# Modulation and the first projection chunks at the start of a two-block fp32 transformer kernel: x and ctx loaded first, modulation matmuls in runs of four groups, and half a chunk more of the projection beside them

## The reference

```python
silu_c = jax.nn.silu(c); silu_cc = jax.nn.silu(c_ctx)
mod = silu_c @ w_mod[l] + b_mod[l]
shift, scale, gate = jnp.split(mod[:, None, :], 3, axis=-1)
cmod = silu_cc @ w_mod[l] + b_mod[l]
cshift, cscale, cgate = jnp.split(cmod, 3)
h = rmsnorm(x, norm_g[l]) * (1.0 + scale) + shift
hc = rmsnorm(cx, norm_g[l]) * (1.0 + cscale) + cshift
u = h @ e_w_in[i]
uc = hc @ e_w_in[i]
```

## Time and profile before

| | |
|---|---|
| median of three runs | 2389.93 us |
| the profiled execution | 2389.53 us |
| its span, first to last instruction | 2387.7 us |
| TensorE matmul busy | 2344.4 us, 98% |
| DVE, ACT, POOL busy | 63%, 44%, 11% |
| granted TensorE clock, mean | 0.996 |

### The profile page before, as it was taken

One profiled execution on the slowest core, in us unless ns is written; L12 is line 12 of the kernel. 1 busy time (PEld: TensorE's weight loads), 2 busy tenths in 40 slices (PEclk: granted clock), 3 DMA queues, 4 the chain that ended last, 5 costly groups with the idle time before them and its releaser, 6 DMA issues. The chain is left out here.

```text
span 2387.7 us, 31243 instructions
## 1 busy us (share of the span) xinstructions
PE 2344.4 (98%) x11532; PEld 1901.8 (80%) x11532; DVE 1502.4 (63%) x2492; ACT 1046.8 (44%) x1755; POOL 270.0 (11%) x404
## 2 busy tenths in 40 slices
PE   6999999999999999999999999999999999999998
PEld 1587888877778788877878889878888888998887
DVE  1379655577777888767646566685675544544655
ACT  3332333344443222524544445445454445654543
POOL 0002120121100000011121001010110001101200
PEclk8999999999999999999999999999999999999999
DMA  9968554444435666575565556765655676667653
GB/s 369 370 219 285 177 162 138 156 168 159 142 115 173 233 198 216 174 266 194 167 214 155 164 194 180 239 212 172 210 171 193 187 222 205 199 190 246 187 196 134
DMA packets 234280, 474.79 MB, mean 199 GB/s; under 512 B 18826, under 2 KB 43720, under 8 KB 233360
## 3 DMA queue, kind: packets, MB, share of 16 engines
q1 hardware_dynamic: 208592, 394.42, 51.0%
q0 software_dynamic: 25248, 77.83, 10.1%
q10 hardware_dynamic: 288, 0.52, 0.1%
HBM read 438.77 MB, written 33.94 MB: 198 GB/s over the span
## 5 line engine op out<-in xcount | busy, mean ns | idle before, releaser
L2301 PE MATMUL pp<-w_hi,hT_hi 128*128 128x512 f32 (+4 forms) x2520 | 1004.1, 398 | 0.5 <-DVE w_lo L1657 0.5
L1657 DVE TENSOR_TENSOR w_lo<-raw,w_hi 128x1024 fp32r<-128x1024 f32 (+4 forms) x568 | 669.8, 1183 | 478.6 <-ACT w_hi L1355 477.1
L2303 PE MATMUL pp<-w_hi,hT_lo 128*128 128x512 f32 (+4 forms) x2520 | 964.2, 383 | 0.0
L2302 PE MATMUL pp<-w_lo,hT_hi 128*128 128x512 f32 (+4 forms) x2520 | 962.4, 382 | 0.0
L1355 ACT ACTIVATE w_hi<-raw 128x1024 fp32r<-128x1024 f32 (+4 forms) x568 | 578.8, 1023 | 444.8 <-PE pp L2303 320.3
L2301 PEld LDWEIGHTS pp<-w_hi,hT_hi 128*128 128x128 f32 x2520 | 474.3, 188 | 101.2 <-issue 23.1
L2303 PEld LDWEIGHTS pp<-w_hi,hT_lo 128*128 128x128 f32 x2520 | 473.3, 188 | 88.8
L2302 PEld LDWEIGHTS pp<-w_lo,hT_hi 128*128 128x128 f32 x2520 | 474.8, 188 | 80.3 <-issue 4.6
L1761 DVE SCALAR_TENSOR_TENSOR arena<-raw,cT,arena 128x512 f32<-128x512 f32 x240 | 170.9, 747 | 1.9
L2296 PE MATMUL pp<-hT_hi,w_hi 128*128 128x512 f32 x384 | 161.3, 420 | 2.8 <-DVE w_lo L1657 2.8
L2298 PE MATMUL pp<-hT_hi,w_lo 128*128 128x512 f32 x384 | 150.3, 391 | 0.0
(11 more groups left out here) (350 smaller groups left out, 1947.3 us busy)
## 6 DMA issues: line engine op xcount, KB each, us to landing
raw<-in_w_in_dram SPq DMA_DIRECT2D x168, 512.0 KB, 4.4
raw<-in_w_mod_dram SPq DMA_DIRECT2D x158, 512.0 KB, 5.2
raw<-in_e_w_in_dram SPq DMA_DIRECT2D x102, 512.0 KB, 5.5
raw<-in_w_o_dram SPq DMA_DIRECT2D x64, 512.0 KB, 4.3
raw<-in_o_w_in_dram SPq DMA_DIRECT2D x64, 512.0 KB, 4.8
raw<-in_w_out_dram SPq DMA_DIRECT2D x64, 512.0 KB, 3.9
raw<-in_w_in_dram SPq DMA_DIRECT2D x56, 440.0 KB, 4.0
arena<-in_w_mod_dram SPq DMA_DIRECT2D x34, 512.0 KB, 11.4
```

What stands on the lines that cost most here:

```text
L1657: dve.tensor_tensor(w_lo[:, g.s % SPLIT, 0:n], raw_of(g)[:, 0:n], w_hi[:, g.s % SPLIT, 0:n].bitcast(F32), ALU.subtract).then_inc(lo_done, 1)
L2301: pe.matmul(dst, hT_hi[:, kk, o:o + P], hi[:, k, :], start=a, stop=False)
L2302: pe.matmul(dst, hT_hi[:, kk, o:o + P], lo[:, k, :], start=False, stop=False)
L2303: ins = pe.matmul(dst, hT_lo[:, kk, o:o + P], hi[:, k, :], start=False, stop=z)
```

## The change

The start is put in another order by a new function, `startup`:

- The loads of x and ctx stand ahead of the first weight load; the squares, the root and the scaling of x move 8 slots ahead.
- Scale and shift of the same quarter share one PSUM bank, Y: four rows at each of the four places, two of scale and two of shift. For that the stationary operand is four columns wide, with two of them zero (`cT` grows from 2 to 6 columns). One `evac` and one `cols` serve both chunks; `cols` now transposes the 112 rows of `parts` (four transposes), and DVE adds up the places by two reductions and adds the bias by two additions. The selector matrix leaves the constants (816 to 512 columns), and only layer 0's bias is loaded at the start.
- `b_q1` is cut in two halves of 256 columns, two quanta for each group. The first, `b_q1a`, runs beside `b_q0`: one K pair is now 2 + 4 quanta. Its two banks are X0 and X1.
- Modulation groups come in runs of four (8 K tiles) with two or three quanta between the runs, by the table `after`. The first projection quantum stands behind 18 modulation groups instead of 24.
- The loads of both chunks are put five loads ahead (two for their first group). 13 buffers serve up to `b_kv`.
- Ahead of the last modulation group stand 31 quanta instead of 20; ahead of `b_kv` stand 64 quanta in both, so `b_kv` begins at slot 128 in both.
- The second half of the chunk, still called `b_q1`, has two quanta in a group, so its split stands at the earliest five slots ahead of its use, where that of `b_q1` stood eleven.
- The `mac`s of the side chunks begin at slot 105 instead of 100, and all side chunks end 4 to 29 slots later; the halves of the store buffer `ust` are swapped in later chunks with two token tiles.

The diff, cut to what the prediction speaks of:

```diff
-EARLY = 3
+EARLY = 5
 LEAD = 3
 
-NMOD, BIAS0 = 24, 98
+NMOD, BIAS0 = 12, 100
...
-            g.split_at = max(self.cut[n - SPLIT].q1 if n >= SPLIT else 0, self.groups[max(0, g.n - AHEAD)].q0 + 1)
+            g.split_at = max(self.cut[n - SPLIT].q1 if n >= SPLIT else 0, self.groups[max(0, g.n - AHEAD - (g.ch.name in ("b_q0", "b_q1a") and 0 < g.j < 6))].q0 + 1)
...
-            self.loads.insert(max(0, len(self.loads) - (EARLY if g.ch.name == "b_q0" else 0)), g)
+            self.loads.insert(max(0, len(self.loads) - ((2 if g.j == 0 else EARLY) if g.ch.name in ("b_q0", "b_q1a") and g.j < 6 else 0)), g)
...
-        first = next(n for n, g in enumerate(self.loads) if g.ch.name == "b_q1")
+        first = next(n for n, g in enumerate(self.loads) if g.ch.name == "b_kv")
         for n, g in enumerate(self.loads):
             g.n = n
-            g.slot = n % (RAW + MORE) if n < first else (n - first) % RAW
+            g.slot = (n - first) % (RAW + MORE) if n < first else (n - first) % RAW
...
+    def startup(self, scale0, shift0, *beside):
+
+        pending, queue = [], []
+
+        def begin(j):
+            for ch in beside:
+                g = Group(len(self.groups), ch, j, len(self.slots))
+                self.groups.append(g)
+                if not ch.groups:
+                    self.chunks.append(ch)
+                    self.C[ch.name] = ch
+                    ch.q0 = g.q0
+                ch.groups.append(g)
+                pending.extend((g, t) for t in range(ch.T))
+
+        def some(n):
+            for _ in range(n):
+                if queue and not pending:
+                    begin(queue.pop(0))
+                if pending:
+                    self.quantum(*pending.pop(0))
+
+        after = (((16, 0),), ((2, 1), (2, 2), (4, 2), (4, 3), (4, 3)), ((4, 3), (4, 2), (4, 3), (4, 3)), ((4, 3), (4, 3), (4, 3), (4, 0)))
+        for n in range(4):
+            parts = [(ch[n], j) for ch in (scale0, shift0) for j in range(8)]
+            for i, (mods, quanta) in enumerate(after[n]):
+                for ch, j in parts[0:mods]:
+                    self.put(ch, j)
+                parts = parts[mods:]
+                if n and i == 0:
+                    queue += [2 * n - 2, 2 * n - 1]
+                some(quanta)
+        queue += [6, 7]
+        while queue or pending:
+            some(1)
...
-        slot, used = C["b_q1"].q0 + 4, 0
+        slot, used = C["shift0_3"].q1 + 10, 0
...
-        b_q0, b_q1 = (Chunk(n, "u", "e_w_in", c, 512, 4, flip="q", dst="b_q", dcol=c - 3072, pieces=3) for n, c in (("b_q0", 3072), ("b_q1", 3584)))
+        b_q0, b_q1a, b_q1 = (Chunk(n, "u", "e_w_in", c, w, w // 128, flip="q", dst="b_q", dcol=c - 3072, pieces=3)
+                             for n, c, w in (("b_q0", 3072, 512), ("b_q1a", 3584, 256), ("b_q1", 3840, 256)))
         b_kv = Chunk("b_kv", "u", "e_w_in", 4096, 512, 4, dst="u0")
-        for n in range(4):
-            for m, ch in enumerate((scale0[n], shift0[n])):
-                self.run(ch)
-                if n:
-                    self.put(b_q0, 2 * n - 2 + m)
-        for j in (6, 7):
-            self.put(b_q0, j)
+        self.startup(scale0, shift0, b_q1a, b_q0)
...
-                ch.bank = [("Y", "X1")[n % 2]]
-                n += 1
+                ch.bank = ["Y"]
+                continue
+            if ch.name == "b_q1a":
+                ch.bank, ch.half = ["X0", "X1"], [1]
...
-                add(ch.end[t], "evac", ch.name, t)
+                if ch.kind != "mod" or ch.name.startswith("shift"):
+                    add(ch.end[t], "evac", ch.name, t)
                 if ch.kind == "u" and t % 2:
                     add(ch.end[t] + 1, "store", ch.name, t // 2)
-            if ch.kind == "mod":
-                add(ch.q1 + (7 if ch.name in early else 1 if ch.name == "shift0_3" else 3), "cols", ch.name)
+            if ch.kind == "mod" and ch.name.startswith("shift"):
+                add(ch.q1 + (0 if ch.name == "shift0_0" else 1), "cols", ch.name)
...
-            add(12 + t, "sq_x", t)
-        add(17, "sums", "n0", 0)
-        add(17, "root", "n0", 0)
-        add(18, "x_scale", 0)
-        add(18, "x_scale", 1)
+            add(4 + t, "sq_x", t)
+        add(9, "sums", "n0", 0)
+        add(9, "root", "n0", 0)
+        add(10, "x_scale", 0)
+        add(10, "x_scale", 1)
         for n in range(4):
             for k in range(4):
-                add(C[f"shift0_{n}"].q1 + (3 + k if n < 3 else 1 + k // 2), "x_turn", 0, 4 * n + k, 0)
+                add(C[f"shift0_{n}"].q1 + ((1, 1, 1, 3) if n == 0 else (2, 3, 7, 8) if n < 3 else (2, 2, 4, 5))[k], "x_turn", 0, 4 * n + k, 0)
...
-        add(W.C["b_q1"].q0 - 6, "clear")
+        add(W.C["shift0_3"].q1 + 3, "clear")
...
-                        use(("X0", "O")[K % 2], *e)
+                        use({1: "X0", 2: "X1", 12: "Y", 14: "Y"}.get(K, "O"), *e)
...
-        cT = sb("cT", [P, KT_, 2])
+        cT = sb("cT", [P, KT_, 6])
...
-                if g.n == RAW:
+                if g.n == 0:
...
-                act.activation(cT[:, :, :], pY[:, 0:32].rearrange("p (v k) -> p k v", v=2), ACT.Copy).then_inc(freed["Y"], 1)
+                act.wait_ge(cleared, 2)
+                act.activation(cT[:, :, 2:4], pY[:, 0:32].rearrange("p (v k) -> p k v", v=2), ACT.Copy).then_inc(freed["Y"], 1)
...
             def cols(name):
-                block = C[name].block
                 key = ("cols", name)
                 dve.wait_ge(filled["O"], left["O", key])
-                dve.tensor_copy(mod_cols[:, block:block + 4, :], pO[:, 0:8].rearrange("p (a b) -> p a b", b=2)).then_inc(freed["O"], 1)
-                scaled_gain(name, key)
+                row_groups = pO.rearrange("p (a r n) -> p a n r", a=4, r=4)
+                for v0, one in ((2, name), (0, name.replace("shift", "scale"))):
+                    own.link(dve.tensor_reduce(mod_cols[:, C[one].block:C[one].block + 4, :], row_groups[:, :, v0:v0 + 2, :], AX.X, ALU.add))
+                for one in (name, name.replace("shift", "scale")):
+                    m = BIAS0 + C[one].c0 // 512
+                    block = mod_cols[:, C[one].block:C[one].block + 4, :]
+                    ins = dve.tensor_tensor(block, block, pO.rearrange("p (a n) -> p a n", a=4)[:, :, m:m + 1].broadcast_to([P, 4, 2]), ALU.add)
+                ins.then_inc(freed["O"], 1)
+                scaled_gain(name.replace("shift", "scale"), key)
...
-            first_users = {"b_q0", "out0_0", "c_q0", "c_kv", "q_b0", "kv_b0", "out1_0", "idx0", "out2_0", "g0", "out3_0"}
+            first_users = {"b_q1a", "out0_0", "c_q0", "c_kv", "q_b0", "kv_b0", "out1_0", "idx0", "out2_0", "g0", "out3_0"}
...
+                shift = ch.name.startswith("shift")
+                if g.j == 0 and not shift:
                     begin(ch.bank[0], "acc", ch.name, 0)
                 b = bank[ch.bank[0]]
                 for k, K in enumerate(g.ks):
                     r = 32 * (K % 4)
-                    ins = pe.matmul(b[r:r + 2, :], cT[:, K, :], raw_of(g)[:, 512 * k:512 * k + 512], start=K < 4, stop=K >= 12)
+                    ins = pe.matmul(b[r:r + 4, :], cT[:, K, 0:4] if shift else cT[:, K, 2:6], raw_of(g)[:, 512 * k:512 * k + 512],
+                                    start=K < 4 and not shift, stop=K >= 12 and shift)
...
                 b = begin("O", "cols", name)
-                n = mod_n[name]
-                pe.wait_ge(*freed_from(C[name].bank[0], ("acc", name, 0)))
-                pe.wait_ge(bias_here, 32)
-                m = 12 * C[name].layer + C[name].c0 // 512
-                p, pick = parts[0:BIAS0 + NMOD, :], keep[0:BIAS0 + NMOD, C_SEL + 2 * m:C_SEL + 2 * m + 2]
+                pe.wait_ge(*freed_from("Y", ("acc", name.replace("shift", "scale"), 0)))
+                pe.wait_ge(bias_here, 16)
+                r = BIAS0 + NMOD
                 for k in range(4):
-                    ins = pe.matmul(b[:, 2 * k:2 * k + 2], p[:, 128 * k:128 * k + 128], pick, start=True, stop=True)
+                    ins = pe.transpose(b[:, 128 * k:128 * k + r], parts[0:r, 128 * k:128 * k + 128], ident[0:r, 0:r])
```

More of the change, by code:

```diff
@@ L711, in turns @@
                 g, t = self.W.slots[q]
-                if g.j == 0:
+                if g.j == 0 and not (g.ch.kind == "mod" and g.ch.name.startswith("shift")):
                     take(g.ch.bank[t], "acc", g.ch.name, t, fills=False)
@@ L1084, in setup @@
                 pool.memset(half_neg, -0.5).then_inc(setup_done, 1)
-                for l in range(2):
-                    pool.dma_start(parts[BIAS0 + 12 * l:BIAS0 + 12 * l + 12, :], D["b_mod"][l].rearrange("(c n) -> c n", n=512)).then_inc(bias_here, 16)
+                pool.dma_start(parts[BIAS0:BIAS0 + NMOD, :], D["b_mod"][0].rearrange("(c n) -> c n", n=512)).then_inc(bias_here, 16)
                 pool.wait_ge(setup_done, 1)
@@ L1154, in tables @@
                     for g in W.lent:
-                        if g.ch.kind == "mod":
-                            pool.wait_ge(quanta, g.q1)
```

(9 more changed lines are left out.)

24 lines of the change are left out of this document (7 added, 17 removed).

## The result

The changed kernel took 2397.62 us (median of 5 runs, 2396.54 to 2403.31) against 2389.93 (2387.28 to 2390.55). The ratio is 1.0037, 95% interval 1.0025 to 1.0049: slower by 0.25 to 0.5%, where I had forecast 2380.3 and faster. The profiled execution took 2396.54 with a span of 2394.7, 7.0 longer than the one before.

A forecast was written before the change was run, and what follows sets the result against it. TensorE was taken to bound the kernel, so the gain is b_kv's move from 178.3 to 168.2 us, 10.1, less 0.6: 9.5. 2389.53 - 9.5 = 2380.0 for the profiled run, 2380.3 as median; range 2376.0 to 2386.0.

The forecast's parts named there:

- What bounds the kernel, and the start: Whole kernel: TensorE is the limit, with DMA close to it up to 115.4 us; the gain is b_kv's move.
- parts 2 and 3: Start: first quantum at 46 us instead of 53.3, then a slot-by-slot walk to b_kv at 168.2.
- the 9.5 I took: Gain at b_kv: 10.1 us from the walk, less 0.6 for a bank, a split and a buffer that could be late.
- One term in it: Start: the last modulation landing at 114.9 us, with 1.355 us for 512 KB and half for b_q1a's groups.
- the 4.8 us in hand: End of the modulation: the walk's last run ends at 119.7 us, 4.8 behind the last landing at 114.9.
- rival 4: Behind b_kv: late splits or folds make TensorE wait and give back 5 to 9 us, 2385.3 to 2389.9; chance 0.08.
- Rivals 1, 2 and 3: Start: DMA-limited throughout, 2376.1, chance 0.10; O, ACT and DVE waits, 2384.9, 0.17; clock stays down, 2395.3, 0.05.
- the last part: Signs of being right or wrong; b_kv to the end was to take 2208.2 us - 1.3 for fold_row, within 1.

The follow-up runs named there:

- e12: The changed kernel with the pause in the side multiply-adds before c_q0 beginning at slot 602 instead of 601: 2381.42 us.
- e1: The changed kernel with the side multiply-adds starting at slot 100 instead of 105 and the clearing of parts two slots sooner: 2381.88 us.
- e9: The changed kernel with the side multiply-adds starting at slot 104 instead of 105: 2394.11 us.
- e8: The changed kernel with the side multiply-adds starting at slot 103 instead of 105: 2383.55 us.
- e13: The changed kernel with the pause in the side multiply-adds before c_q0 beginning at slot 604 instead of 601: 2395.76 us.

## Why the prediction was wrong

- *What bounds the kernel, and the start*: right. The first quantum and b_kv came within 0.5 us of parts 2 and 3 (46.51, 168.70), the end of the last modulation run 1.3 late (120.96 for 119.7), and the 9.5 I took is the 9.6 seen. One term in it was too small: the last modulation weights landed at 119.10 and not at 114.9. Five loads landed 1.8 to 3.3 us behind the one before them (at 53.20, 82.13, 84.31, 110.62 and 117.73) instead of 1.36, and why is open. TensorE came to their run at 119.06, so of the 4.8 us in hand only 0.9 were left (119.10 + 0.96 is 120.06, and the run ended at 120.96); that b_kv didn't move with it was luck. The granted clock fell to half for 3.4 us at 41.5, ahead of the first quantum, and held at 1.00 behind it, as I had taken it. The Trainium skill (TensorE: Matmul & The Clock Gate, "HAM oscillation — how this bites in real kernels") says that waiting for DMA between short stretches makes the clock swing. This trace shows no swinging in the start, only these 3.4 us; near 990 us, behind splits that are late by 4 us, it shows 10.2 us at 1.2 GHz.
- *The step that failed* is the sentence "TensorE's work from there on differs only by where a few small operations stand, the change is worth what it moves b_kv". TensorE's work is the same, but not its waits. The start slot of the side work is a part of the change, and I priced it only in rival 4, as side chunks "4 to 29 slots later" that make folds late, 5 to 9 us with a chance of 0.08. The larger loss is at another place: a buffer was held over the pause at 601 to 611 and four weight loads of c_q0 and c_kv went out too late. The smaller one, 4.0 us by the trace, is of the kind that rival 4 named, a row of the side work that is summed up and stored late. Together they cost 16.2 us by the medians (2397.62 against e12's 2381.42), about twice the rival's price.
- Rivals 1, 2 and 3 didn't happen. TensorE was busy for 52.97 of the 53.30 us ahead of b_kv, so DVE didn't hold it up, and its matmuls waited 1.0 us in sum ahead of a `cols` and never ahead of a turn behind the first quantum.
- Two slips: the last part subtracts fold_row's 1.3 from the stretch behind b_kv, where it has to be added (it stands behind b_kv in the changed kernel). The forecast itself has it right. And rival 4's upper end, 2380.3 + 9, is 2389.3 and not 2389.9. The stretch behind b_kv, named there as a sign of being wrong, is the one that showed it.
- With both places mended the forecast holds: 2381.42 (e12) and 2381.88 (e1) against 2380.3. Some 1.3 us trickle away between b_kv and 985. Behind that e1 loses 0.7 (8.8 ahead of the kernel before near 987, 8.1 at the end). The profiled execution of e12, the slowest of its five, loses 3.1 (8.9 and 5.8), most of it between 1060 and 1206, and I haven't followed where.

What I could have read before any run is the plan: the changed kernel's load order and slots stand in its code, and the lead of every load can be listed without a chip. I walked the start slot by slot and took everything behind it as before.

## What to carry to other kernels

When a change shifts the start of a stream of background work, follow the stream to its end through every pause of its plan: a unit of work that a pause cuts in two keeps its buffer for the length of the pause, and in a queue with a fixed order all later loads stand behind it. List for each load the distance from the last release its queue must have seen to its use, before and after, and look at the smallest: here c_q0 and c_kv ran free with a least lead of 6 slots, and with 1 they cost 10.6 us (e9 against e8) and 14.3 us (e13 against e12), far away from the edit. Look at the other end of the stream as well: its last result stored at slot 732, one slot behind an operation that needed the place, cost some 4 us more. A gain at the start of a kernel that TensorE bounds does reach the end, if nothing behind it is planned from what was moved.
